# One first stage for all modulation, layer 0's norm and the time-step projection; the rest of the time steps moved into the state-space prologue, the bias table into the output stage

## The reference

```python
def reference(x, c, ctx, c_ctx, ada_w, ada_b, pre_g, post_g, ssd_w_in, ..., na_rpb, na_w_out):
    D = D_MODEL                                   # 1024
    sc_l, sc_c = jax.nn.silu(c), jax.nn.silu(c_ctx)
    for i in range(DEPTH):                        # 2
        mod_l = sc_l @ ada_w[i] + ada_b[i]        # ada_w[i] is 1024 x 3072
        mod_c = sc_c @ ada_w[i] + ada_b[i]
        shift_l, scale_l, gate_l = (mod_l[:, None, :D], mod_l[:, None, D:2 * D], mod_l[:, None, 2 * D:])
        shift_c, scale_c, gate_c = mod_c[:D], mod_c[D:2 * D], mod_c[2 * D:]
        h_l = _rms(x, pre_g[i]) * (1.0 + scale_l) + shift_l
        h_c = _rms(ctx, pre_g[i]) * (1.0 + scale_c) + shift_c
        ...                                       # mixer: _ssd_mixer (layer 0) or _na_mixer (layer 1)
        x = x + gate_l * _rms(out_l, post_g[i])
        if i < DEPTH - 1:
            ctx = ctx + gate_c * _rms(out_c, post_g[i])
    return x

def _ssd_mixer(h_l, h_c, w_in, conv_w, conv_b, dt_bias, a_log, d_skip, norm_g, w_out, ctx_out):
    # proj: t = h @ w_in; its last 64 columns are the time steps
    #   dt = jax.nn.softplus(dt + dt_bias); A = -jnp.exp(a_log); then dt*A is summed up within chunks
    ...
def _na_mixer(h_l, h_c, w_in, rpb, w_out, ctx_out):
    # bias = rpb[:, roff, coff], -inf outside a window of 16 columns
    ...
```

## Time and profile before

| | us |
|---|---|
| median of 3 runs (lowest to highest) | 2570.71 (2567.81 to 2574.24) |
| the profiled execution | 2571.34 |
| its span in the profile | 2569.3 |
| from the start to the state-space stage (stages 1 to 3) | 183.4 |
| from there to its first projection | 7.9 |
| its prologue of 12 units | some 65 |

### The profile page before, as it was taken

One profiled execution on the slowest core, in us unless ns is written; L12 is line 12 of the kernel. 1 busy time (PEld: TensorE's weight loads), 2 busy tenths in 40 slices (PEclk: granted clock), 3 DMA queues, 4 the chain that ended last, 5 costly groups with the idle time before them and its releaser, 6 DMA issues. The chain is left out here.

```text
span 2569.3 us, 36389 instructions
## 1 busy us (share of the span) xinstructions
PE 2258.7 (88%) x12794; PEld 1811.3 (70%) x12794; DVE 1490.7 (58%) x3267; ACT 1122.4 (44%) x2838; POOL 612.8 (24%) x594
## 2 busy tenths in 40 slices
PE   5769999989999998989886799759999999999686
PEld 1318777778787877878674678647788787877465
DVE  1554595968769595977848422162545554555442
ACT  1414564736465463746544311153444444444321
POOL 0012443535344352635333000021111111110000
PEclk8889999999999999999987899969999999999798
DMA  7561001010100101010000643131112121211153
GB/s 248 201 179 48 33 18 50 17 50 25 42 26 17 50 26 41 26 42 26 29 9 25 218 131 99 50 116 42 49 59 67 50 55 53 66 50 42 44 165 94
DMA packets 117260, 172.05 MB, mean 67 GB/s; under 512 B 27577, under 2 KB 78009, under 8 KB 116825
## 3 DMA queue, kind: packets, MB, share of 16 engines
q1 hardware_dynamic: 117080, 169.73, 21.3%
HBM read 141.53 MB, written 30.13 MB: 67 GB/s over the span
## 5 line engine op out<-in xcount | busy, mean ns | idle before, releaser
L599 PE MATMUL sg_pP<-h_h_hi,sg_whi 128*128 128x512 f32 (+1 forms) x1152 | 417.1, 362 | 14.2 <-POOL sg_wlo L1042 14.2
L600 PE MATMUL sg_pP<-h_h_lo,sg_whi 128*128 128x512 f32 (+1 forms) x1152 | 411.4, 357 | 0.0
L601 PE MATMUL sg_pP<-h_h_hi,sg_wlo 128*128 128x512 f32 (+1 forms) x1152 | 411.0, 357 | 0.0
L599 PE MATMUL at_pP<-h_h_hi,at_whi 128*128 128x512 f32 (+1 forms) x640 | 254.0, 397 | 13.2 <-POOL at_wlo L1837 13.2
L599 PEld LDWEIGHTS sg_pP<-h_h_hi,sg_whi 128*128 128x128 f32 x1152 | 221.9, 193 | 44.7 <-POOL sg_wlo L1042 14.3
L600 PEld LDWEIGHTS sg_pP<-h_h_lo,sg_whi 128*128 128x128 f32 x1152 | 221.6, 192 | 30.2
L601 PEld LDWEIGHTS sg_pP<-h_h_hi,sg_wlo 128*128 128x128 f32 x1152 | 221.1, 192 | 30.6
L601 PE MATMUL at_pP<-h_h_hi,at_wlo 128*128 128x512 f32 (+1 forms) x640 | 238.6, 373 | 0.0
L600 PE MATMUL at_pP<-h_h_lo,at_whi 128*128 128x512 f32 (+1 forms) x640 | 237.2, 371 | 0.0
L1837 POOL TENSOR_TENSOR at_wlo<-at_wr,at_whi 128x1024 fp32r<-128x1024 f32 x32 | 76.3, 2385 | 564.9 <-ACT at_whi L1747 564.9
L1385 PE MATMUL op_pa<-op_whi,op_yhi 128*128 128x512 f32 x448 | 144.6, 405 | 51.5 <-DVE op_ylo L1442 51.5
(11 more groups left out here) (226 smaller groups left out, 4908.1 us busy)
## 6 DMA issues: line engine op xcount, KB each, us to landing
sg_wr<-in_w_ssd SPq DMA_DIRECT2D x48, 512.0 KB, 3.4
at_wr<-in_w_na SPq DMA_DIRECT2D x32, 512.0 KB, 3.5
at_bias<-bt SPq DMA_DIRECT2D x256, 64.0 KB, 2.3
op_yr<-y SPq DMA_DIRECT2D x10, 1024.0 KB, 7.5
md_mod_w<-in_ada_w SPq DMA_DIRECT2D x4, 2048.0 KB, 13.4
nt_mod_w<-in_ada_w SPq DMA_DIRECT2D x4, 2048.0 KB, 10.2
ts_mod_w<-in_ada_w SPq DMA_DIRECT2D x4, 2048.0 KB, 14.8
y<-sg_Z SPq DMA_DIRECT2D x16, 512.0 KB, 3.0
```

The source lines that it names most:

```text
L599: pe.matmul(out, w_hi[:, k, :], h_hi[:, k, t0:t0 + n], start=(k == 0), stop=False)
L600: pe.matmul(out, w_hi[:, k, :], h_lo[:, k, t0:t0 + n], start=False, stop=False)
L601: x = pe.matmul(out, w_lo[:, k, :], h_hi[:, k, t0:t0 + n], start=False, stop=(k == KT - 1))
```

## The change

Stages 1 to 3 become one, `first_stage` (tiles `fs_`).
- Modulation is loaded as 24 slabs of 128 rows of `ada_w` (1 MB each, a ring of four) in three rounds of eight: layer 0's shift and scale, both layers' gates, layer 1's shift and scale. `csil` is padded from 2 to 32 columns, and the four matmuls of a slab write to four strips of 32 partitions of one bank: `pacc[32*j:32*(j+1)]`.
- The norm of layer 0 runs beside the first round. The transposed tiles stay in `xT`; scale and shift are applied later, block by block, by ACT (`h_hi`) and DVE (`h_lo`). `w_dt` is split there too, and the three blocks of the time-step projection lie between the slabs of rounds two and three. The first state-space weight tile is also loaded and split there.
- The time steps' ten transposes come ahead of unit 0 in the state-space stage; the vector chain is cut in pieces at the head of prologue steps 1 to 5, 9 and 10 of DVE; the four matmuls of the sums stand ahead of unit 7 on PE. The tables of groups 0 and 1 are copied straight to `tab`; those of groups 2 to 7 are stored from `Z` and `hb`. They were packed by 12 copies, and are by 36 smaller ones.
- The 64 gathers lie in SP's queue behind the loads of weight tiles 6 to 13. The bias table is masked in eight pieces of 128x480 elements in `out_project` of layer 0: two loads, a POOL addition and two stores a tile.

The diff, cut to its core:

```diff
 class Modulation:
+    NB = 4
+    RING = 4
+    def load(self, sp, k, wld, at):
+        done = 0
+        for layer, lo, hi in self.sources:
+            sp.dma_start(self.w[:, (at + k) % self.RING, done:done + hi - lo],
+                         self.a["ada_w"][layer, k * P:(k + 1) * P, lo:hi]).then_inc(wld, 16)
+            done += hi - lo
+    def products(self, pe, k, at):
+        for j in range(self.NB):
+            x = pe.matmul(self.pacc[32 * j:32 * (j + 1), :], self.csil[:, k, :],
+                          self.w[:, (at + k) % self.RING, j * self.NC:(j + 1) * self.NC],
                           start=(k == 0), stop=(k == KT - 1))
+        x.then_inc(self.slab, 1)
...
+def first_stage(nc, a, x_in, h_hi, h_lo, pre, pad_dram, mod_rows, mod_cols, kept):
...
+        @block.sync
+        def _(sp):
+            def slab(n):
+                if n >= RING:
+                    sp.wait_ge(rounds[(n - RING) // KT].slab, (n - RING) % KT + 1)
+                rounds[n // KT].load(sp, n % KT, wld[n % RING], n // KT * KT)
...
+        @block.vector
...
+            for b, (t0, n) in enumerate(BLOCKS):
+                for k in range(KT):
+                    s = xT[:, k, t0:t0 + n]
+                    dve.wait_ge(hi, KT * b + k + 1)
+                    if k < KT - KA:
+                        dve.tensor_scalar(s, s, gain[:, k, v:v + 1], mc[:, k, v:v + 1], ALU.mult, ALU.add).then_inc(lo, 1)
...
+                    dve.tensor_tensor(h_lo[:, k, t0:t0 + n], s, h_hi[:, k, t0:t0 + n].bitcast(F32),
+                                      ALU.subtract).then_inc(hl, 1)
...
+        @block.tensor
...
+            for k in range(KT):
+                modulate(k)
+                turn(k)
+            turn(KT)
+            pe.wait_ge(rw, 1)
...
+            for n in range(KT, KT + 3):
+                modulate(n)
+            time_steps(0)
+            for n in range(KT + 3, KT + 7):
+                modulate(n)
+            time_steps(1)
+            for n in range(KT + 7, KT + 10):
+                modulate(n)
+            time_steps(2)
+            for n in range(KT + 10, 3 * KT):
+                modulate(n)
...
 def ssd_groups(...):
+                if 6 <= w < 14:
+                    gather_runs(sp, pad_dram, run_dram, range((w - 6) * NRUN, (w - 5) * NRUN), run)
                 if kind == "z" and i == PAIRS - 1 and g >= 1:
                     store(g - 1)
...
+            pe.wait_ge(small, 128)
+            for c in range(NCH):
+                x = pe.transpose(pturn[c // HALF][...], raw[0:H2, c * P:(c + 1) * P], ident[0:H2, 0:H2])
             for q in range(PRO):
+                if q == SUMS:
+                    pe.wait_ge(tch, 16)
+                    ... # four matmuls
                 unit(q)
...
             for step in range(PRO):
+                time_steps(step)
                 if at(step, 1) is not None:
                     conv(at(step, 1))
...
 def out_project(nc, a, layer, y_dram, kt, w_dram, tiles, mod_rows, st_o, runs=None):
+                if runs and t >= 1:
+                    i = t - 1
+                    if 1 <= i <= PIECES:
+                        sp.wait_ge(tad, i)
+                        ... # two stores of piece i - 1
+                    if i < PIECES:
+                        if i:
+                            sp.wait_ge(bst, 32 * i)
+                        ... # two loads of piece i
```

More of the change, by code:

```diff
@@ new lines, in first_stage @@
+        mhalf = m.sb("mhalf", [P, 1])
+        rows = m.sb("rows", [P, Modulation.NC])
+        gbias = m.sb("gbias", [P, Modulation.NC])
+        grow = m.sb("grow", [P, Modulation.NC])
+        bcol1 = m.sb("bcol1", [P, 2 * KT])
+        mc1 = m.sb("mc1", [P, 2 * KT, 2])
+        preg = m.sb("preg", [P, KT])
+        bcol = m.sb("bcol", [P, 2 * KT])
+        mc = m.sb("mc", [P, 2 * KT, 2])
+        gain = m.sb("gain", [P, KT, 2])
+        ident = m.sb("ident", [P, P])
+        pt = [m.ps(f"pt{i}") for i in range(4)]
@@ new lines, in _ @@
+            sp.dma_start(craw[:, :, :], a["cvec"]).then_inc(cld, 16)
+            for t in range(NCH):
+                if t >= RX:
+                    sp.wait_ge(tr, t - RX + 1)
+                sp.dma_start(xt(t), x_in(t)).then_inc(ld[t], 16)
+                if t == 0:
+                    sp.dma_start(ident[:, :], a["ident"]).then_inc(small, 16)
+                    sp.dma_start(preg[:, :], a["pre_g"][0]).then_inc(small, 16)
+                    sp.dma_start(bcol[:, :], a["ada_bc"][0]).then_inc(small, 16)
+                if t >= 2:
+                    slab(t - 2)
@@ L213, in _ @@
                 sp.dma_start(prow[i][:, QC:QC + DC], a["rpb"][i * NR // 2:(i + 1) * NR // 2, :]).then_inc(rld, 16)
+            for n in range(KT, 2 * KT):
+                slab(n)
             sp.wait_ge(rld, 32)
@@ new lines, in _ @@
+            pe.wait_ge(sil, 4)
+            pe.wait_ge(small, 48)
+            for k in range(KT):
+                modulate(k)
+                turn(k)
+            turn(KT)
+            pe.wait_ge(rw, 1)
+            for k in range(4):
+                y = pe.transpose(pcol[:, k * P:(k + 1) * P], rows[:, k * P:(k + 1) * P], ident[:, :])
+            y.then_inc(tn, 1)
+            turn(KT + 1)
+            pe.wait_ge(ka, NCH)
+            pe.wait_ge(kd, NCH)
+            for n in range(KT, KT + 3):
+                modulate(n)
@@ new lines, in _ @@
+            time_steps(0)
[7 more added lines that the diff above has]
+                modulate(n)
+            pe.wait_ge(crw, 1)
+            for k in range(4):
+                y = pe.transpose(pcol[:, k * P:(k + 1) * P], rows[:, k * P:(k + 1) * P], ident[:, :])
+            y.then_inc(mtn, 1)
@@ L259, in norm_transpose @@
+def norm_transpose(nc, a, layer, x_in, mod_cols, h_hi, h_lo):
     R = 4
     KA = 4
-    N = len(chunks)
-    steps_after = [[j for j in range(N * KT) if 1 + j * (NCH - 1) // (N * KT) == t] for t in range(NCH)]
-    ends_after = [[j // KT for j in steps if j % KT == KT - 1] for steps in steps_after]
     with ExitStack() as ctx:
@@ L282, in norm_transpose @@
         ld = [m.sem(f"ld{i}") for i in range(R)]
-        mod = Modulation(nc, m, a, csil, chunks, N, mod_rows, mod_cols) if N else None
-        run = m.sem("run")
-        runs = range(NRUN0, NRUN1)
         block = ctx.enter_context(nc.Block())
@@ L753, in _ @@
             store(G - 1)
+            sp.wait_ge(run, 16 * CB * QC)
             for b in range(NBL):
@@ L1311, in _, with out_project @@
                 norm_late(G - 1, c)
-def out_project(nc, a, layer, y_dram, kt, w_dram, tiles, mod_rows, st_o):
+def out_project(nc, a, layer, y_dram, kt, w_dram, tiles, mod_rows, st_o, runs=None):
     NH = D // 2
```

703 lines of the change are left out of this document (368 added, 335 removed).

## The result

The changed kernel takes 2486.66 us (median of 4 runs, 2484.67 to 2489.82) beside 2569.26 us for the kernel before on the same chip; the ratio is 0.968, 95% interval 0.9657 to 0.9703. The forecast was 2486. A second set of runs of the same two kernels gave 2489.71 us (2481.65 to 2495.68) and 0.9683 (0.966 to 0.9706).

The account below looks back on a forecast made before the run. It took transfers to bound most of the new first stage and PE the prologue. Unit 0 89.0 us earlier, +2.4 and +1.6 in the prologue, sum to -85.0 from 2571.34, said as 2486 us; 8-in-10 range 2477 to 2505.

Parts of the forecast that it names:

- Transfers: First stage: loading 31.5 MB at 381 GB/s takes 82.6 us, so the last slab arrives no earlier than about 85.6 us.
- Four strips at once: First stage on PE: a slab's four matmuls run together, 0.86 us a slab, 21 us in all.
- rival 1: First stage: the strips don't overlap, so matmuls run one after another; +37 us, 2523 us in total; chance 0.07.
- Up to the eighth slab: First stage, round one: eighth slab arrives at T = 39 us; PE's work per slab hides behind 4.1 us of transfers.
- Three queues: After the eighth slab (time T, 39 us): transfers, DVE's `h_lo` and PE's blocks run beside each other; last slab at 87 us.
- 1 to 2 us for the ring's wait of slab 22: First stage: slab 22 is issued only when slab 18 is done, just before the queue runs dry; costs 1 to 2 us.
- Constants, 7.1 us: Start of the state-space stage: its small constants are there after 7.1 us, and unit 0 starts 8.3 us after the stage.
- Prologue, +2.4 and +1.6: State-space prologue: the sums' matmuls add 2.4 us on PE; DVE waiting for POOL during the copies adds 1.6 us.
- Gathers 0, pieces 0: SP's 64 gathers and the output stage's eight bias-table pieces add 0 us; bounds for the pieces 0 and 10 us.
- 2 mostly false: Rival on the first stage: PE at half clock through rounds two and three; +12 us, 2498 us; chance 0.10.
- rival 3: Output stage: slow round trips of bias-table pieces delay `y` loads; 2606 us at 25 us a round trip; chance 0.02.
- rival 4: Prologue: DVE's chain lands on PE's path, the two-unit cover failing at seven steps; 22 us, 2508 us; chance 0.04.

Follow-up runs that it names:

- e3_blocks_last: Changed kernel with all three blocks of the time-step projection moved from between the slabs to behind slab 23 on PE; 2508.35 us, 0.9768 of the kernel before.
- e1_full: Changed kernel with every slab matmul at 128 weight columns into the whole bank, so none run together, and four x tiles for five; 2540.32 us, 0.9889 of before.
- e8_rx4: Changed kernel holding four tiles of x in place of five, nothing else; 2500.57 us, 0.9739 of the kernel before.
- e7_mask_long: Changed kernel with POOL adding the mask 24 times to each piece of the bias table; 2625.89 us, 1.0201 of the kernel before.
- e6_chain_more: Changed kernel with DVE's prologue chain lengthened by 19.6 us of repeats whose results are overwritten; 2507.36 us, 0.9745 of the kernel before.

## Why the prediction was right, and where not

The total is right (2486 for 2486.66), partly by terms that cancel.

- **Transfers:** 31.5 MB at 381 GB/s, last slab at 85.6 at the earliest. Right within 2 us: 380 GB/s in the sample, and the last slab there at 84.0 in e3_blocks_last.
- **Four strips at once, 0.86 us a slab:** right, 0.93 to 1.06. Shown by the series 3.70, 1.94, 1.06 and by e1_full, whose cost against its control (35.9) is the one of rival 1 (37). The prediction's own evidence was weaker than it said: 70 ns a record for 107 is less than two at once. So the strips carry some 36 us of the gain, 83 at unit 0; no run takes apart what else makes it up.
- **Up to the eighth slab, "hidden either way":** 41 for 39 in this trace, 39.0 to 39.8 in the other three with this code, so right within the scatter, but on less room than I thought. x's five tiles wait for the transposes, and slabs stand behind them; I had not looked at SP's wait on `tr`, and e8_rx4 shows how steep it is, 6.1 us for one tile less.
- **Three queues:** block 0 at T + 15 (14), block 1 at T + 23.3 (22 to 23), block 2 at T + 34.4 (33). 7 us for a block at half clock was too much, both large ones ran at full clock in 5.6 us. PE waited for DVE's `h_lo` once, 4.7 us, ahead of block 0, with all four slabs landed: the prediction had named that as a sign of being wrong, though its own times for block 0 imply it, and it is part of what leaves the ring full.
- **"1 to 2 us for the ring's wait of slab 22":** mis-sized. The gaps cost 4 to 6 us in all (last slab there at 87.6 to 89.8, against 84.0 in e3_blocks_last). The last slab is through at T + 50.7, and not at T + 49 as 87 us and its 1 us of matmuls have it; the rest of the difference is T.
- **End of the stage, 7 us:** from 89.8 (last slab's matmuls start) to 96.8, 7.0. Right.
- **Constants, 7.1 us:** wrong, 9.95. The whole row of issues took 5.4 us from the stage's start to the last one's end (one issue alone 1.73), and the landing behind it another 4.5. This is the largest single miss on the path, 2.9 us, and the 8.3 us of the seam became 11.2. Together with the stage's end (96.8 for 94) this makes the -89.0 a -83.3.
- **Prologue, +2.4 and +1.6:** together 4.0 for 3.1 measured. The sums are 8 records that take 0.27 us each, as I took them, and PE waits once for DVE, 1.2 us at the end, behind the copies. DVE's busy time went from 27.1 to 50.2 us, 23 for the 22 I had. Three operations beside POOL's four splits were long: a convolution's second half (L1179, 2.77 us where it takes 0.75), another's first (L1176, 2.23 for 0.49) and the first pair of copies (2.39). I had allowed four such waits.
- **Gathers 0, pieces 0:** right as far as a trace shows it. Group 0's stores now go out at 325.8 to 327.5 and ACT first overwrites `Z` at 340.8, still 13 us later; the output stage's products took 231.7 us for 232.9.
- **What made up for it:** -83.3 + 3.1 is -80.2 and not -85.0; the profiled execution's groups ran 3.9 us shorter than those of the one before, and the output and attention stages 0.9 us. That doesn't belong to the change: in the other execution of the changed kernel the groups took 8.1 us more. So the median agrees with the forecast better than its working does, by some 5 us, and that part of the agreement is luck.

Of the rivals, 1 is shown false (its price shown right), 2 mostly false: the granted clock was 0.83 to 1.00 in rounds two and three, half clock for single stretches (56.5 to 59.9, and from 87.2, where PE waited for slabs 22 and 23). The Trainium skill, TensorE: Matmul & The Clock Gate, HAM oscillation, tells of a PE that falls back to half clock at every wait for its next slice of data, in a kernel whose waits are longer than those here, which are at most 2.7 us once the first slab is there; so, other than the prediction says, it does not make this rival the forecast. The traces agree with it in part: PE waited 1.6 and 2.7 us ahead of the seventh and eighth slab and ran both at full clock (1.07 us), waited 1.9 and 0.5 us ahead of the last two and ran them at half (1.94); in e8_rx4 three slabs of round one came after waits of 3.0 to 4.0 us, and all three ran at half (1.93 to 1.94); and with slabs alone on PE the granted clock was 0.50 (e3_blocks_last, 60 to 75 us). What decides was not tested. Rivals 3 and 4 are false at the sizes of this kernel. e7_mask_long and e6_chain_more show that both mechanisms exist; rival 3 had too little slack, 10 us for the 21.8 of a tile, and rival 4's threshold was not located.

## What to carry to other kernels

Two columns of weights leave TensorE almost empty: give independent products of few columns their own strips of the output's partitions, and four run in about the time of one (1.06 us for 3.70 one after another). When a stage is bound by its transfers, count them in its one queue in order: a load that waits for its buffer holds everything behind it, and loads of small rows belong where no large load waits, behind the last one, or into the stage before if the next one's start depends on them. Where a stage's code is unchanged but its time moves by 8 us between executions, read small effects at a milestone ahead of it, and measure that milestone's own scatter first (2.7 us here).
